# Moving the long convolution's filter spectra into the first MLP and its steps between the branch_a tiles

## The reference, cut to what matters

```python
def fft_long_conv(u, k_spec, skip):
    L = u.shape[1]
    uf = u.astype(jnp.float32)
    y = jnp.fft.irfft(jnp.fft.rfft(uf, n=2 * L, axis=1) * k_spec[None], n=2 * L, axis=1)[:, :L]
    return (y + uf * skip.astype(jnp.float32)).astype(u.dtype)

def hyena(z, conv_w, conv_b, w1, b1, w2, b2, freq, w3, skip):
    z = short_conv(z, conv_w, conv_b)
    v, x1, x2 = jnp.split(z, HY_ORDER + 1, axis=-1)
    filt = hyena_filters(z.shape[1], w1, b1, w2, b2, freq, w3)
    y = v
    for n, gate in enumerate((x1, x2)):
        k_spec = two_sided_spectrum(filt[:, 0, n], filt[:, 1, n])
        y = gate * fft_long_conv(y, k_spec, skip[n])
    return y
```

## Time and profile before

| | |
|---|---|
| time, median of 3 runs | 2651.36 us |
| the profiled execution's own time | 2652.18 us |
| its span | 2650.4 us |
| TensorE matmul busy | 2540.4 us, 96% |
| VectorE busy | 1692.4 us, 64% |
| ScalarE busy | 1026.2 us, 39% |
| GpSimd busy | 16.5 us, 1% |
| mean granted TensorE clock | 0.975 |
| DMA, mean over the span | 205 GB/s |

### The profile page before, as it was taken

How to read it: one execution, slowest core, us unless ns; L and a number is a source line. 1 busy time by engine, 2 the same in 40 slices (tenths; PEclk the granted TensorE clock), 3 DMA queues, 4 the chain that set the end, 5 groups by cost and what they waited for, 6 DMA issues and landing times.

```text
span 2650.4 us, 35356 instructions
## 1 busy us (share of the span) xinstructions
PE 2540.4 (96%) x15666; PEld 2218.9 (84%) x15666; DVE 1692.4 (64%) x1586; ACT 1026.2 (39%) x928; POOL 16.5 (1%) x36
## 2 busy tenths in 40 slices
PE   6998999999999999799999998979899999999998
PEld 6998888888888888699999995468688888888886
DVE  5477567777777777756656764456766665555655
ACT  4154454334334343444444341124343343343432
POOL 0000000000000000000000000000000000000000
PEclk8799999999999999899999999889999999999999
DMA  5233356787777877765666662024545555555552
GB/s 215 87 120 128 119 180 233 297 321 270 307 296 280 322 276 285 281 223 211 234 240 252 240 253 72 4 96 168 197 165 190 194 183 192 189 190 193 189 190 111
DMA packets 77544, 542.93 MB, mean 205 GB/s; under 512 B 8650, under 2 KB 10869, under 8 KB 12496
## 3 DMA queue, kind: packets, MB, share of 16 engines
q1 hardware_dynamic: 74976, 529.82, 54.4%
q0 software_dynamic: 2416, 10.86, 1.1%
HBM read 538.55 MB, written 2.10 MB: 204 GB/s over the span
## 4 chain that ended last, share of the span: by engine, by line
PE 86%; DVE 6%; ACT 3%; DMA 2%; issue 2%; SPq 0%; POOL 0%; DVEq 0%; ACTq 0%
PE ps L472 16%; PE ps L485 10%; PE ps L487 10%; PE ps L486 10%; PE ps L473 8%; PE ps L451 7%; PE ps L452 7%; PE ps L453 7%; DMA stage<-wstream 2%; ACT w_hi L876 2%; DVE w_lo L1227 1%; PE ps L832 1%; PE ps L824 1%; PE ps L812 1%; PE ps L639 1%
## 5 line engine op out<-in xcount | busy, mean ns | idle before, releaser
L1227 DVE TENSOR_TENSOR w_lo<-stage,w_hi 128x2048 fp32r<-128x2048 f32 x403 | 922.1, 2291 | 548.1 <-ACT w_hi L876 546.3
L876 ACT ACTIVATE w_hi<-stage 128x2048 fp32r<-128x2048 f32 x403 | 769.4, 1913 | 827.2 <-DMA stage<-wstream 334.4
L472 PE MATMUL ps<-xs,w_hi 128*128 128x512 f32 x1920 | 681.2, 398 | 0.9 <-DVE w_lo L1227 0.9
L473 PE MATMUL ps<-xs,w_lo 128*128 128x256 f32 x1920 | 539.5, 281 | 0.0
L472 PEld LDWEIGHTS ps<-xs,w_hi 128*128 128x128 f32 x1920 | 361.1, 188 | 87.6 <-DVE w_lo L1227 1.9
L487 PE MATMUL ps<-w_lo,hs 128*128 128x512 f32 x1024 | 398.4, 389 | 0.0
L486 PE MATMUL ps<-w_hi,hs 128*128 128x512 f32 x1024 | 398.4, 389 | 0.0
L485 PE MATMUL ps<-w_hi,hs 128*128 128x512 f32 x1024 | 398.3, 389 | 0.0
L473 PEld LDWEIGHTS ps<-xs,w_lo 128*128 128x128 f32 x1920 | 363.1, 189 | 2.5
L451 PE MATMUL ps<-xs,w_hi 128*128 128x256 f32 x1152 | 327.4, 284 | 0.0
L453 PE MATMUL ps<-xs,w_lo 128*128 128x256 f32 x1152 | 326.7, 284 | 0.0
(11 more groups left out here) (366 smaller groups left out, 2805.5 us busy)
## 6 DMA issues: line engine op xcount, KB each, us to landing
stage<-wstream SPq DMA_DIRECT2D x499, 1024.0 KB, 4.8
xraw<-xT SPq DMA_DIRECT2D x4, 512.0 KB, 9.2
resid<-x SPq DMA_DIRECT2D x2, 1024.0 KB, 13.2
out<-out_t SPq DMA_DIRECT2D x4, 512.0 KB, 3.0
c_row<-c_row POOLq DMA_DIRECT2D x1, 1024.0 KB, 5.2
w<-w POOLq DMA_DIRECT2D x8, 128.0 KB, 3.1
fn_row<-fn_row POOLq DMA_DIRECT2D x1, 1024.0 KB, 5.1
bo_row<-bo_row POOLq DMA_DIRECT2D x1, 1024.0 KB, 7.0
```

The costliest lines, as they stand in the source:

```text
L472: pe.matmul(o2, hi, rhs[:, k, :], start=(first and j == 0), stop=False)
L473: mm = pe.matmul(o2[:, S:2 * S], lo, rhs[:, k, 0:S], start=False, stop=False)
L876: act.activation(w_hi[:, w % HIGH, :], stage[:, n % RING, :], ACT.Copy).then_inc(hi_ready, 1)
L1227: tt(w_lo[:, slot, :], stage[:, slot, :], f(w_hi[:, w % HIGH, :]), ALU.subtract).then_inc(lo_ready, 1)
```

## The change

- The filter work (the two small products, `filters`, the window, `filter_spectrum`, the copy from PSUM) is done during the first MLP. The small products go behind tiles a=8 and a=12 of it, and filter i behind tile a = 20 + 12i with its spectrum five tiles later. VectorE's three operations are in the three tiles after the filter. Each spectrum (1 MB) is written to DRAM (`spectra`) by GpSimd's queue, and loaded again in branch_a.
- TensorE's part of a convolution step is dealt out between the branch_a tiles. These tiles now use one PSUM bank each (`column_by_column`), so that banks 1 and 3 are free for `back`.
- The frequencies are k + 1/2, so that no frequency lacks a sine: `dft_u`, `nyq` and `k_nyq` go.
- The loops of the diff stand in this order: GpSimd's queue, TensorE's `filter_work` (called behind each tile w = 43 + a of the first MLP), ScalarE and VectorE in the first MLP, then TensorE, ScalarE and VectorE in branch_a.
- The first two branch_b tiles each run in two halves; the 24 `ada` tiles of z come in the first 60 of its tiles; many buffers have new places.

```diff
         if step >= T_Z:
-            due = 72 + (step - T_Z + 1) // 3
+            due = 72 + min(24, (step - T_Z + 1) * 2 // 5)
...
+    def filter_tile(i):
+        return T_MLP1 + 20 + 12 * i
+    def conv_bank(i, c):
+        b = 4 + c // 2 if i == 3 else 1 + 2 * (c // 2)
+        return ps[:, b, (c % 2) * S:(c % 2) * S + S]
...
         load_w3(0)
+        for i in range(4):
+            if i < 3:
+                pool.wait_ge(sem("filters_made"), i + 1)
+                load_w3(i + 1)
+            pool.wait_ge(sem("spectrum_taken"), i + 1)
+            pool.dma_start(spectra[i], k_made[:]).then_inc(sem("spectrum_stored"), 16)
...
+        pool.wait_ge(tile_done, T_BA)
+        for i in range(4):
+            if i >= 2:
+                pool.wait_ge(sem("y_made"), i - 1)
+            pool.dma_start(k_spec[i % 2][:], spectra[i]).then_inc(sem(f"spectrum_loaded_{i}"), 16)
...
+        def filter_work(a):
+            if a == 8:
+                pe.wait_ge(sem("hid_loaded"), 48)
+                pe.matmul(ps[0:64, 4, 0:S], w1[:], feats[:], start=True, stop=True).then_inc(sem("hid_pre"), 1)
+            if a == 12:
+                pe.wait_ge(sem("hid_sin"), 1)
+                pe.matmul(ps[0:64, 4, 0:S], w2[:], hid[:], start=True, stop=True).then_inc(sem("hid_pre"), 1)
+            for i in range(4):
+                if a == filter_tile(i) - T_MLP1:
+                    pe.wait_ge(sem("hid_sin"), 2)
+                    pe.wait_ge(sem("w3_loaded"), 32 * (i + 1))
+                    if i:
+                        pe.wait_ge(sem("spectrum_taken"), i)
+                    for d in range(2):
+                        for j in range(2):
+                            mm = pe.matmul(ps[:, 4 + 2 * d + j, :], hid[:, j * P:j * P + P], w3[:, d, :], start=True,
+                                           stop=True)
+                    mm.then_inc(sem("filters_made"), 1)
+                if a == filter_tile(i) - T_MLP1 + 5:
+                    pe.wait_ge(sem("filters_added"), i + 1)
+                    pe.wait_ge(sem("dft_loaded"), 16)
+                    for m in range(4):
+                        for j in range(2):
+                            mm = pe.matmul(ps[:, 4 + m, :], dft[:, j, m * P:m * P + P], h_sd[:, m // 2, j, :],
+                                           start=(j == 0), stop=(j == 1))
+                    mm.then_inc(sem("spectrum_made"), 1)
...
+            for i in range(4):
+                if w == filter_tile(i) + 6:
+                    act.wait_ge(sem("spectrum_made"), i + 1)
+                    if i:
+                        act.wait_ge(sem("spectrum_stored"), 16 * i)
+                    act.activation(k_made[:], ps[:, 4:8, :], ACT.Copy).then_inc(sem("spectrum_taken"), 1)
...
+            for i in range(4):
+                if w == filter_tile(i) + 1:
+                    dve.wait_ge(sem("filters_made"), i + 1)
+                    dve.wait_ge(sem("win_ready"), 2)
+                    if i:
+                        dve.wait_ge(sem("spectrum_made"), i)
+                    link(tt(filt[:], ps[:, 4:8, :].rearrange("p (d j) c -> p d j c", d=2),
+                            win[:, i % 2].unsqueeze(1).broadcast_to([P, 2, 2, 512]), ALU.mult))
+                if w == filter_tile(i) + 2:
+                    tt(h_sd[:, 0], filt[:, 0], filt[:, 1], ALU.add)
+                if w == filter_tile(i) + 3:
+                    tt(h_sd[:, 1], filt[:, 0], filt[:, 1], ALU.subtract).then_inc(sem("filters_added"), 1)
...
-        filters(0)
         turn_input(0)
-        filter_spectrum(0)
-        input_spectrum(0)
-        filters(1)
-        back(0)
-        filter_spectrum(1)
-        filters(2)
-        for i in range(1, 4):
-            turn_input(i)
+        tile(T_BA, y_a)
+        for i in range(4):
             input_spectrum(i)
+            tile(T_BA + 2 * i + 1, y_a)
             if i < 3:
-                filter_spectrum(i + 1)
+                tile(T_BA + 2 * i + 2, y_a)
+                turn_input(i + 1)
             back(i)
-            if i < 2:
-                filters(i + 2)
-        for w in range(T_BB, T_WO):
-            tile(w, y_b, (lambda g: (sem("yb_split"), g + 1)) if w == T_BB else None)
+        for half in range(2):
+            pe.wait_ge(sem("yb_split"), half + 1)
+            for w in range(T_BB, T_BB + 2):
...
+                mm = weights_moved(w, y_b, 4 * half, 4, u, 1024 * half, half == 0, half == 1, None)
...
         def take_yb(half):
             act.wait_ge(sem("conv_out"), 3 + half)
+            act.wait_ge(sem("u_spectrum"), 4)
...
+        for w in range(T_BA, T_BB):
+            if (w - T_BA) % 2 == 0 and w > T_BA:
+                split(w + 2)
+                take_input((w - T_BA) // 2)
+            elif w == T_BA:
+                take_input(0)
+                split(w + 2)
+            else:
+                split(w + 2)
+            if w == T_BB - 1:
+                take_yb(0)
+        take_yb(1)
...
+        for w in range(T_BA, T_BB):
+            split(w + 2)
+            l = w - T_BA
+            if l % 2:
+                multiply(l // 2)
+            u = U_BA + l
+            summed(dve, u, w)
+            c = 2 * l
+            took_done(tt(mixacc[:, c:c + 2, :], mixacc[:, c:c + 2, :], one_bank(u), ALU.mult), u)
+            if l in (2, 4, 6):
+                gate(l // 2 - 1)
+        gate(3)
...
-    turn = 2 * math.pi * np.outer(lags, np.arange(S)) / (2 * S)
+    turn = 2 * math.pi * np.outer(lags, np.arange(S) + 0.5) / (2 * S)
```

More of the change, by code:

```diff
@@ L129, in begins @@
     kind, u, k0 = job(w)
-    return kind in ("half", "pair") or k0 == 0 or T_WOUT <= w < T_MLP1 and k0 == 8
+    return kind in ("column", "half", "pair") or k0 == 0 or T_WOUT <= w < T_MLP1 and k0 == 8
 def ends(w):
@@ L292, in _program @@
[L292 to L310, removed]
+    sgw = at("sgw", [P, SGUC, P], F32, H)
+    sgb = at("sgb", [P, SGUC, P], F32, H + 4 * K)
@@ new lines, in _program @@
+    hid_n = at("hid_n", [64, S], F32, Z + 22 * K)
+    feats = at("feats", [33, S], F32, Z + 23 * K)
+    w1 = at("w1", [33, 64], F32, Z + 24 * K)
+    w2 = at("w2", [64, 64], F32, Z + 24 * K + 256)
+    k_made = at("k_made", [P, 4, 512], F32, Z + 28 * K)
+    w3 = at("w3", [64, 2, 512], F32, Z + 36 * K)
+    hid = at("hid", [64, S], F32, Z + 48 * K)
+    X0 = 64 * K
+    k_spec = [at(f"k_spec{b}", [P, 4, 512], F32, X0 + 8 * K * b) for b in range(2)]
+    y_b = at("y_b", [P, SGUC, 2 * S], F32R, X0 + 16 * K)
@@ L311, in _program @@
+    y_spec = at("y_spec", [P, 4, 512], F32, X0 + 24 * K)
+    dft_in = at("dft_in", [P, 2, 512], F32, Z + 40 * K)
+    idft = at("idft", [P, 4, S], F32, Z + 44 * K)
+    u_tok = at("u_tok", [P, 2, 512], F32, X0 + 16 * K)
+    prod = [at("prod0", [P, 512], F32, o + 3104), at("prod1", [P, 512], F32, Z + 48 * K)]
+    spectra = nc.dram_tensor("spectra", (4, P, 4, 512), F32, kind="Internal").ap()
     ps = ctx.enter_context(nc.psum_tensor("ps", [P, 8, 512], F32))
@@ L401, in _ @@
         pool.dma_start(c_row[:], dram["c_row"]).then_inc(sem("c_loaded"), 16)
[L403 to L407, removed]
+        pool.wait_ge(sem("cond_made"), 1)
         pool.dma_start(feats[:], dram["feats"]).then_inc(sem("hid_loaded"), 16)
@@ L488, in tokens_moved, with column_by_column @@
             return mm
+        def column_by_column(w, rhs, u):
+            for c in range(2):
+                for k in range(SGUC):
+                    a = (k * 2 + c) * P
+                    o2 = one_bank(u)[:, c]
+                    hi, lo = w_hi[:, w % HIGH, a:a + P], w_lo[:, place(w) % RING, a:a + P]
+                    pe.matmul(o2, hi, rhs[:, k, 0:S], start=(k == 0), stop=False)
+                    pe.matmul(o2, hi, rhs[:, k, S:2 * S], start=False, stop=False)
+                    mm = pe.matmul(o2, lo, rhs[:, k, 0:S], start=False, stop=(k == SGUC - 1))
+            return mm
         def tile(w, rhs, ready=None, hook=None):
@@ L770, in _ @@
         pe.wait_ge(sem("sgu_done"), 1)
[L771 to L793, removed]
         def turn_input(i):
@@ L798, in turn_input @@
             if i:
-                pe.wait_ge(sem("conv_out"), i)
+                pe.wait_ge(sem("y_made"), i)
+            if n:
+                pe.wait_ge(sem("conv_out"), i - 1)
+            else:
+                pe.wait_ge(evac_done, U_Z + 26 + 2 * half)
             for c in range(4):
@@ L803, in turn_input @@
             mm.then_inc(sem("u_turned"), 1)
[L805 to L817, removed]
         def input_spectrum(i):
+            pe.wait_ge(sem("dft_in_loaded"), 16)
             pe.wait_ge(sem("u_ready"), i + 1)
@@ L1063, in _ @@
                 m_hi(3)
+            a = w - T_MLP1
+            if a in (11, 16):
+                act.wait_ge(sem("hid_arg"), 1 if a == 11 else 2)
+                act.activation(hid[:], hid_a[:], ACT.Sin).then_inc(sem("hid_sin"), 1)
+            if a == 14:
+                act.wait_ge(sem("delta_loaded"), 16)
+                for j in range(NB):
```

(18 more changed lines are left out.)

166 lines of the change are left out of this document (65 added, 101 removed).

## The result

The changed kernel takes 2612.45 us, the median of 4 runs (2610.82 to 2613.49), the one before 2651.22 beside it. The ratio is 0.9854, with a 95% interval of 0.9837 to 0.9872. That is 38.8 us less, where 43.4 were predicted (2651.4 to 2608), and inside the range of 2598 to 2636. The profiled execution took 2613.49, with a span of 2611.5 against 2650.4.

What follows compares the result with a forecast made beforehand. TensorE bounds the first MLP; between branch_a and branch_b the lone convolution steps' waits and slow matmuls do. 2652.2 - 89.5 (rebuilt stretch) + 42.1 (work moved into the MLP) + 4 (stalls) = 2608.8, median 2608; range 2598 to 2636.

Steps and rivals of the forecast that it cites:

- TensorE's prices: Convolution work on TensorE: eight transposes 0.87 (0.9 taken), input_spectrum 6.87, back 6.92 us, from the earlier trace.
- the cycle: Branch_a's steady part: two tiles, a turn, back and the next input_spectrum take 26.2 us, three times 78.6.
- The cover: Branch_a cycles: two tiles and the turn hide VectorE's multiply with 4.8 us to spare, so handshakes cost nothing.
- rival D: Branch_a cycles not covered: VectorE late, TensorE idles some 3 us, back 2.3 slower; +16, 2624; chance 0.10.
- The tail: After the last input_spectrum: take_yb(0)'s wait puts back 12.2 us later, TensorE idles 6.4, back takes 9.26.
- branch_b: Branch_b: VectorE-ScalarE loop of 6.72 us a tile, 37.6 from first to last w_lo, sets w_o's start at 74.1.
- The term for stalls: First MLP: 4 us of stalls, about one slack for each of four filters and four stores.
- A: First MLP gives back more: VectorE's 25 us and half of the stores' 13 exposed; +28, 2636; chance 0.12.
- B: First MLP's weight stream stays late over 108 tiles, 0.6 us more each; +65, 2669, slower; chance 0.07.
- Spectra late: Branch_a: side-by-side loads at 8.4 per half MB land the first spectrum 20.1 us late; +22, 2630; chance 0.05.
- E: Convolution steps stand alone as before, so only nyq's 6.9 us are gained; 2644.5; chance 0.02.
- The rate in z: In z, earlier ada tiles raise DMA to 243 GB/s, below the 314 had, costing nothing.

Runs made afterwards that it cites:

- experiment 3: Changed kernel with extra 512-wide products on VectorE in each of multiply(0) to multiply(2): 2613.38 us with 4, 2632.21 us with 10.
- experiment 4: Changed kernel with y_b over the two k_spec buffers instead of u_tok, so take_yb doesn't wait for the last input_spectrum: 2606.14 us, ratio 0.9829.
- Experiment 6: Changed kernel with the small products and their chains moved from up to down tiles of the first MLP, filters nine tiles later: 2611.63 us, ratio 0.9848.
- experiment 5: Changed kernel storing only 64 bytes of each partition of a spectrum, with weight tiles loaded in the spectra's place: 2613.02 us.
- experiment 1: Changed kernel with the convolution steps behind the eight branch_a tiles instead of between them, filters still in the first MLP: 2645.54 us.
- experiment 2: Kernel before with only the half-integer frequencies (no nyq, no dft_u, one spectrum copy instead of four): 2638.5 us, ratio 0.9961.
- experiment 8: Changed kernel with ScalarE in branch_b copying a tile's result behind the next w_hi, not ahead of it: 2608.87 us.
- experiment 9: Changed kernel with y_b on the k_spec buffers, small products in down tiles and ScalarE's new branch_b order together: 2596.15 us, ratio 0.9789.

## Why the prediction was right, and by what it was off

The forecast for the profiled execution was 2608.8, and it took 2613.49: 4.7 too low. The mechanism held in the rebuilt stretch. In the first MLP the total of the stalls came near and their place didn't.

- *TensorE's prices* from the earlier trace rows held: 0.87, 6.87 and 6.91. So did the first part, 13.66 against 13.5, and the cycle, 26.16 against 26.2. The last `input_spectrum` ended 92.15 us after the start, against 92.1.
- *The cover.* Steps 0 to 2 cost no waiting, as said, and rival D (+16) was refuted; experiment 3 shows the point from which it decides. But the margin was put too high. It was reckoned to `back`, at 4.8; the turn ahead of it waits for `y_made` too, so that only 3.9 are left by the prediction's own durations. It made no difference to the time.
- *The tail* was found in the diff, with its reason: `take_yb(0)`'s wait, and `w_lo` and `multiply(3)` queued behind it. Predicted were 12.2 us to `back` and 6.4 of idle time, measured 12.05 and 6.32; experiment 4 shows that the wait is its cause. `back` then took 10.08, not 9.26: the first mis-sized term, 0.8. A size was taken from one row. Because of this wait the mean granted clock of the stage is 0.95, not the 1.0 that the prediction named as a sign.
- *branch_b.* 37.6 was predicted from the first to the last `w_lo`, and 37.56 measured, with the loop of 6.72 kept. The second miss is a slip: the sum ended at the last `w_lo`, though the earlier trace rows show 1812.48 - 1811.18 = 1.3 us from there to TensorE's start on w_o. It is 1.31 again (1771.35 to 1772.66). With small differences of either sign the two make the stretch's 1.8.
- *The first MLP.* 42.1 + 4 were predicted, 48.1 measured. The 42.1 is right. The term for stalls was 4 and came to 6.0, the largest miss of the sum, 2.0, and it lies elsewhere than the prediction put it, which was four filters and four stores. Up to tile a = 20 the stage is 5.2 longer, of which 0.9 are the small products: 4.3 of stalls from their chains on VectorE and ScalarE, in the up tiles, which the prediction hadn't looked at for slack. Experiment 6 bears this out. The four filters and four spectra with their stores cost 42.9 in all, 1.7 over their own 41.2. So one part was put too high and the other at next to nothing, and that the sum came near is luck. Rivals A and B, which put +28 and +65 on the MLP, were refuted, A's stores by experiment 5. (B's 108 tiles are not all of 5.44 us: 48 of them are up tiles of 5.64 and more. It changes nothing in its 65.)
- *Spectra late* (C): the four loads landed after 6.7, 10.0, 5.8 and 5.7 us. The two issued side by side thus took longer than the later ones, and one longer than the 8.4 of the earlier trace rows. But the first was there at 1612.01, and VectorE took it at 1618.33, right behind `input_spectrum`, with 6.3 us to spare. VectorE was busy for 6.0 of its 6.7 us. The factor of five that the Trainium skill gives (page SBUF — State Buffer, section A bandwidth-pool intuition that's wrong) is for a `tensor_copy` on VectorE; beside the float32 TENSOR_TENSOR, SCALAR_TENSOR_TENSOR and TENSOR_SCALAR operations of this place it did not show, and the 26 us estimated with it are refuted for them.
- *E*: experiment 1 is that case, 2645.54 against the 2644.5 given. It was priced nearly right, by luck: the half-integer frequencies alone were worth 12.4 by the medians (experiment 2, 2650.92 beside it to 2638.5), not 6.9, and experiment 1, with the filters moved and the tiles not dealt out, stands 7.0 above that.
- *The rate in z.* 1.4 MB in 5.76 us is 255 GB/s with 1 MB of 1024 KB (the 3.3 us of a store were reckoned so), not 243. It stays below the 314, and TensorE doesn't idle in z.

The rest, 0.9, lies in the parts up to the first MLP, in z and from w_o on, and is of the size by which these stages differ between executions.

## What to carry to other kernels

Before moving work out of a stage that idles, ask whether it was that stage's cover: here the filters' move with the steps left at one place left TensorE idle for 33.6 us there instead of 26.7, and with tiles dealt out in their place for 6.3. Ask also what the work costs where it goes, 6 to 7 us of stalls over its own length here. When steps are dealt out, follow each engine's queue behind every new wait, buffer addresses included; the two dearest leftovers were one `at(...)` offset (6.9 us) and the order of a copy and a split (6 us). Look for slack in each kind of tile that gets new work, not only in the tightest-looking one.

## What the runs showed of the hardware

The same idle time didn't always cost the same. `back`, 6.91 without a wait, took 10.08 after 6.32 us of idle time in the kernel after, and 8.53 after 6.33 in experiment 8, whose chain of waits has:

```profile
1713.21 8.53 PE ps L871 x32
```

In five more traces with this wait it took 8.85 to 10.02. After 2.35, in experiments 4 and 9, it took 7.14 both times, and the granted clock stayed at 1.00. After the 6.3 us it had fallen to its lower level, 1.2 GHz, in the idle time, and it came back within `back`: 5.9 us from its start in the kernel after (1714.8), 2.8 us from it in experiment 8. Half of these stretches, 3.0 and 1.4, is nearly all of the 3.2 and 1.6 that `back` was longer. The Trainium skill, page TensorE: Matmul & The Clock Gate, section What's actually happening, says that the number of slow matmuls after a start varies from run to run; these rows agree. So such a term wants a range: here 1.6 to 3.2 us.

The load of a function table on ScalarE (1.28 us) between two other operations was no cheap detail, where ScalarE and VectorE hand each tile's result to and fro: with the 2.19 us of the window behind it, TensorE waited 2.46 us for the `w_lo` of a later tile.
